# First and last mixer of an eight-stage transformer: blocks of 512 columns, bank pairs in turns, and a one-pass softmax step

## The reference

```
h = x                                        # (256, 1024)
h = h + moba_mixer(rms_norm(h))              # stage A
h = h + conv_ffn(rms_norm(h))                # F0
h = h + mla_mixer(rms_norm(h))               # B
h = h + conv_ffn(rms_norm(h))                # F1
x = x + pool_mixer(rmsnorm(x))               # POOL
x = x + conv_ffn_2(rmsnorm(x))               # F2
x = x + chunk_attention(rmsnorm(x))          # DD
x = x + conv_ffn_2(rmsnorm(x))               # F3
```

## Time and profile before

| what | value |
|---|---|
| median of 3 runs | 1085.82 us (1085.78 to 1086.26) |
| the profiled execution, own time | 1085.73 us |
| its span, first to last instruction | 1083.9 us |
| PE busy with matmuls | 1076.6 us (99%) |
| PE busy with weight loads (overlap) | 973.2 us (90%) |
| DVE / ACT busy | 854.6 us (79%) / 656.8 us (61%) |
| granted TensorE clock | full speed in every slice |
| mean DMA rate | 177 GB/s |
| share of PE in the chain that ended last | 95% |

### The profile page before, as it was taken

One profiled execution on the slowest core, in us unless ns is written; L12 is line 12 of the kernel. 1 busy time (PEld: TensorE's weight loads), 2 busy tenths in 40 slices (PEclk: granted clock), 3 DMA queues, 4 the chain that ended last, 5 costly groups with the idle time before them and its releaser, 6 DMA issues.

```text
span 1083.9 us, 17571 instructions
## 1 busy us (share of the span) xinstructions
PE 1076.6 (99%) x7218; PEld 973.2 (90%) x7218; DVE 854.6 (79%) x1264; ACT 656.8 (61%) x934; POOL 1.3 (0%) x8
## 2 busy tenths in 40 slices
PE   9999999999999999999999999999999999999998
PEld 9998988888898898888889888888999988888888
DVE  7987689877577888988667999776659878998852
ACT  7656557664467775766456577554458765776540
POOL 0000000000000000000000000000000000000000
PEclk9999999999999999999999999999999999999999
DMA  8643256556436045655553366555555443665540
GB/s 310 221 156 118 97 189 229 210 184 215 149 132 224 2 156 223 233 195 184 213 185 117 122 232 229 185 213 186 176 184 180 142 146 126 226 208 193 208 148 30
DMA packets 31951, 191.74 MB, mean 177 GB/s; under 512 B 4480, under 2 KB 5888, under 8 KB 12032
## 3 DMA queue, kind: packets, MB, share of 16 engines
q1 hardware_dynamic: 31872, 190.63, 50.1%
HBM read 189.56 MB, written 1.05 MB: 176 GB/s over the span
## 4 chain that ended last, share of the span: by engine, by line
PE 95%; DVE 2%; ACT 1%; DMA 1%; issue 0%; SPq 0%; DVEq 0%; ACTq 0%
PE banks L414 20%; PE TB L414 12%; PE banks L416 11%; PE SB L414 10%; PE banks L382 8%; PE banks L384 7%; PE banks L383 7%; PE TB L416 6%; PE SB L416 6%; PE banks L581 2%; PE TB L560 1%; PE SB L547 1%; PE SB L937 1%; PE banks L704 1%; DMA raw<-in_a_qkv 1%; PE SB L942 0%
## 5 line engine op out<-in xcount | busy, mean ns | idle before, releaser
L1541 DVE TENSOR_TENSOR wlo<-raw,whi 128x2048 fp32r<-128x2048 f32 (+2 forms) x180 | 395.2, 2200 | 81.1 <-ACT whi L1071 81.0
L1071 ACT ACTIVATE whi<-raw 128x2048 fp32r<-128x2048 f32 (+2 forms) x180 | 330.3, 1839 | 81.9 <-PE banks L416 28.5
L414 PE MATMUL banks<-xx,whi 128*128 128x512 f32 x704 | 247.3, 391 | 0.0
L416 PE MATMUL banks<-xx,wlo 128*128 128x256 f32 x704 | 198.5, 282 | 0.0
L414 PEld LDWEIGHTS banks<-xx,whi 128*128 128x128 f32 x704 | 132.2, 188 | 27.7
L414 PE MATMUL TB<-xx,whi 128*128 128x512 f32 x384 | 135.5, 390 | 0.0
L416 PEld LDWEIGHTS banks<-xx,wlo 128*128 128x128 f32 x704 | 133.1, 189 | 0.1
L382 PE MATMUL banks<-whi,xx 128*128 128x256 f32 (+2 forms) x400 | 116.6, 292 | 1.0 <-DVE wlo L2072 0.8
L384 PE MATMUL banks<-whi,xx 128*128 128x256 f32 (+2 forms) x400 | 113.5, 284 | 0.0
L383 PE MATMUL banks<-wlo,xx 128*128 128x256 f32 (+2 forms) x400 | 113.4, 284 | 0.0
L414 PE MATMUL SB<-xx,whi 128*128 128x512 f32 x320 | 111.8, 390 | 0.0
(11 more groups left out here) (219 smaller groups left out, 2042.2 us busy)
## 6 DMA issues: line engine op xcount, KB each, us to landing
raw<-in_gate SPq DMA_DIRECT2D x44, 1024.0 KB, 4.8
raw<-in_up SPq DMA_DIRECT2D x44, 1024.0 KB, 4.8
raw<-in_down SPq DMA_DIRECT2D x32, 1024.0 KB, 4.8
raw<-in_down SPq DMA_DIRECT2D x16, 768.0 KB, 4.3
raw<-in_d_qkv SPq DMA_DIRECT2D x12, 1024.0 KB, 4.7
raw<-in_a_qkv SPq DMA_DIRECT2D x9, 1024.0 KB, 5.8
raw<-in_a_o SPq DMA_DIRECT2D x4, 1024.0 KB, 4.8
raw<-in_b_o SPq DMA_DIRECT2D x4, 1024.0 KB, 4.7
```

The source lines that it names most:

```text
L414: e.matmul(po[:, 0:512], wh[:, k, sl], a[:, kk, :, :].rearrange("p w s -> p (w s)"), start=start, stop=stop, skip_group_check=True)
L416: return e.matmul(po[:, 0:256], wl[:, k, sl], a[:, kk, 0, :], start=False, stop=stop, skip_group_check=True)
L1071: e.activation(whi[n % RING][:, 0:nk * w], raw[n % RAW][:, 0:nk * w], ACT.Copy).then_inc(s_hi, 1)
L1541: e.tensor_tensor(wlo[n % RING][:, 0:nk * w], raw[n % RAW][:, 0:nk * w], whi[n % RING][:, 0:nk * w].bitcast(F32), ALU.subtract).then_inc(s ...
```

## The change

All of it concerns stages A and DD, but for `shifted` and `exponentials`, which stage B's attention uses as well.

- **Units and slots.** K and Q of four heads are now side by side as 512 columns, V of eight heads likewise. Six slots (K/Q of g=0, V of pairs 0 to 3, K/Q of g=1, 2, 3, V of pairs 4 to 7) take two units each, one for rows 0 to 511 and one for rows 512 to 1023. Slot i fills two banks, one per 128 tokens; the pair of banks is i mod 2. A matmul has 512 moving columns.
- **Order on PE.** Slots 0 and 1 run whole (`both_halves`), with the norm's sums between them; then a slot's quarters (token half x unit) stand between pieces of attention. A turn-over is eight transposes, written into the two banks that the slot itself occupied, and the slot after next waits for ACT's copies out of these banks. `av_bank` and with it the waits of `values` change to suit.
- **Softmax step.** Four `tensor_tensor_reduce` write mask minus scores and its minimum; `exp` takes scale -1 and the minimum as bias. DD's factor 1/8 goes into q's gain.
- **Start.** The order of the quarter loads, splits and squares follows the new units; the constants are loaded after unit 3; `lo(u + 3)` stands behind the norm on DVE.

```diff
+HEAD_SLOTS = (("kq", 0), ("v", 0), ("kq", 1), ("kq", 2), ("kq", 3), ("v", 1))
+KQ_SLOT, V_SLOT = (0, 2, 3, 4), (1, 5)
...
     def qkv(name):
-        for g in range(4):
-            for part in (1, 0, 2):
-                plan.append((name, part * 4 + g, KD, 256))
+        for part, i in HEAD_SLOTS:
+            for half in range(2):
+                plan.append((f"{name}_{part}", 2 * i + half, 4, 512))
...
+                def row_of(i, h, k):
+                    wh, wl = unit(u + 2 * i + k // 4)
+                    sl = slice(h * 128, (h + 1) * 128)
+                    return three(slot_bank(s, i, h)[:, :], xx[:, k, 0, sl], xx[:, k, 1, sl], wh[:, k % 4, :],
+                                 wl[:, k % 4, :], k == 0, k == KD - 1)
+                def quarter(i, h, part):
+                    if h == 0:
+                        weights_here(u + 2 * i + part)
+                    if part == 0:
+                        if i == 3:
+                            e.wait_ge(s_vv, n_vv(s, 0, h))
+                        else:
+                            e.wait_ge(s_te, n_te(s, {2: 0, 4: 1, 5: 2}[i], 1 - h))
+                        if i >= 4 and h == 1:
+                            e.wait_ge(s_ol, n_pair(s, 2 * i - 7 - (s == DD)))
+                    for k in range(4 * part, 4 * part + 4):
+                        last = row_of(i, h, k)
...
+                both_halves(0)
+                norm_sums(s)
+                both_halves(1)
+                turn_over(0)
+                    quarter(2, 0, 0)
+                    quarter(2, 0, 1)
+                    pair_scores(0)
+                    quarter(2, 1, 0)
+                    quarter(2, 1, 1)
...
             def shifted(s, j, scale, mask):
-                e.scalar_tensor_tensor(out=sc[:, :, :], in0=SB[:, :, 0:384], scalar=scale, in1=mask, op0=ALU.mult,
-                                       op1=ALU.add).then_inc(s_msk, 1)
-                e.wait_ge(s_msk, n_pair(s, j))
-                e.tensor_reduce(mxs[:, 0:2], sc[:, :, 0:128], AX_X, ALU.max)
-                kept(e.tensor_reduce(mxs[:, 2:4], sc[:, :, 128:384], AX_X, ALU.max))
-                after_own()
-                e.tensor_scalar(nms, mxs, -1.0, None, ALU.mult).then_inc(s_nmx, 1)
+                for a in range(2):
+                    for h, sl in HALVES:
+                        last = e.tensor_tensor_reduce(sc[:, a, sl], SB[:, a, sl], mask[:, a, sl], -scale, 3e38, ALU.add,
+                                                      ALU.min, low[:, 2 * h + a:2 * h + a + 1])
+                last.then_inc(s_msk, 1)
```

More of the change, by code:

```diff
@@ L444, in last_pair @@
                         last.then_inc(s_half, 1)
[L446 to L454, removed]
             def token_sums(src, dst):
@@ L653, in as_it_comes @@
[L653 to L663, removed]
-                        if (i, k) == (1, 6):
-                            norm_sums(s)
-                    last.then_inc(s_used, 1)
@@ L706, in turn_over @@
-                    last.then_inc(s_turn, 1)
+                    for q in range(2):
+                        b = slot_bank(s, KQ_SLOT[g], q)
+                        if s == DD and q == 1 and g >= 2:
+                            e.wait_ge(s_ol, n_pair(s, 2 * g - 3))
+                        for c in range(2):
+                            at = q * 256 + c * 128
+                            for h in range(2):
+                                last = e.transpose(b[:, c * 256 + h * 128:c * 256 + (h + 1) * 128],
+                                                   nkq[:, h, at:at + 128], ident)
+                        last.then_inc(s_turn, 1)
@@ new lines, in heads_mixer @@
+                    quarter(2, 0, 0)
[3 more added lines that the diff above has]
+                    quarter(2, 1, 1)
+                    pair_scores(1)
+                    quarter(3, 0, 0)
+                    quarter(3, 0, 1)
+                    turn_over(1)
+                    transposes(s, 0)
+                    quarter(3, 1, 0)
+                    quarter(3, 1, 1)
+                    values(s, 0)
+                    transposes(s, 1)
@@ new lines, in heads_mixer @@
+                    pair_scores(2)
+                    quarter(4, 0, 0)
+                    quarter(4, 0, 1)
+                    values(s, 1)
+                    turn_over(2)
+                    transposes(s, 2)
+                    pair_scores(3)
+                    quarter(4, 1, 0)
+                    quarter(4, 1, 1)
+                    values(s, 2)
+                    transposes(s, 3)
+                    pair_scores(4)
+                    quarter(5, 0, 0)
+                    quarter(5, 0, 1)
@@ L751, in heads_mixer @@
+                    values(s, 3)
+                    turn_over(3)
                     transposes(s, 4)
-                    half(3, 2, 1, range(4))
+                    pair_scores(5)
+                    quarter(5, 1, 0)
+                    quarter(5, 1, 1)
+                    transposes(s, 5)
                     pair_scores(6)
-                    half(3, 2, 1, range(4, KD))
+                    rows(0)
+                    values(s, 4)
+                    pair_scores(7)
+                    rows(1, 2)
@@ L804, in heads_mixer @@
-                attention_tail(s, u + 12)
+                    rows(3)
+                    transposes(s, 6)
+                    rows(4)
+                    project(s, u + 12, 2, range(2))
+                    values(s, 6)
+                    transposes(s, 7)
+                    rows(5)
+                    project(s, u + 12, 2, range(2, 4))
+                    values(s, 7)
+                    rows(6)
+                    project(s, u + 12, 2, range(4, 6))
+                    rows(7)
+                    project(s, u + 12, 2, range(6, 8))
@@ L1234, in natural @@
                     e.wait_ge(s_rc, COL[s])
                     if g:
[L1236 to L1241 removed]
+                        e.wait_ge(s_turn, n_turn(s, 2 * g - 1))
```

673 lines of the change are left out of this document (320 added, 353 removed).

## The result

| | before | after |
|---|---|---|
| median, us | 1085.86 (1085.59 to 1086.26, 20 runs) | 1083.63 (1083.15 to 1085.42, 20 runs) |
| profiled execution, own time | 1085.73 | 1083.64 |
| its span | 1083.9 | 1081.8 |
| PE / DVE / ACT busy | 1076.6 / 854.6 / 656.8 | 1074.4 / 833.3 / 654.8 |

The ratio is 0.9981, 95% interval 0.9974 to 0.9988: 2.1 us, and the interval reaches from 1.3 to 2.8 us. The forecast of 1083.6 is met; how it was met is another matter, and most of this part is about that. The medians of the experiments leave out five slow executions, which took 1317 to 5170 us; the intervals are of ratios to the kernel before, run beside each.

The account below looks back on a forecast made before the run. PE, 99% busy, was taken to bound the kernel. Longer matmuls -1.96, gaps -3.5, switches -0.45 and new waits +3.85 summed to -2.1 us, from 1085.73 to 1083.6 us; range 1080.7 to 1087.0.

Parts of the forecast that it names:

- 1. longer matmuls: PE in A and DD: 512-column matmuls replace pairs of 256, winning 3.4 ns per pair, -1.96 us in all.
- 2a. start: Stage A's first 90 matmuls: 1.33 us of PE gaps go, one new wait of 0.5 us comes.
- 2b. wait for Q: Scores of pair 6 in stage A no longer wait for ACT's copy of Q, -0.9 us.
- 2c. rows behind `output_lo(6)`: Projection row after six transposes no longer waits for `output_lo(6)`: 0.45 us in A, 0.80 in DD.
- 3. switches: Fewer PE returns from transposes to projection, 21 to 14 in A, 21 to 16 in DD: -0.45 us.
- 4. norm's sums: Stage A after slot 0: PE newly waits for the last sum of squares, +0.85 us.
- 4. copy of K, A and DD: After `turn_over(0)`, PE waits for ACT to copy V twice, then K: +1.1 us in A, +0.75 in DD.
- 4. DD's chain before transposes 2: After DD's third scores, PE waits for DVE's work through normalization 2, +0.65 us.
- stage A near 117.5 and DD near 116.5 us: Sign expected in the profile after: these lengths for the two rewritten stages, from 119.35 and 117.02 us.
- DVE is not the bound: Softmax step falling from 2.12 to 1.6 us per pair on DVE was worth nothing by itself.
- the slow rival: DVE becomes the bound in A and DD, with a 3.3 us softmax step: +6.9 us, 1090.5 us, chance 0.13.
- the pipeline is later: Margins of 0 to 1 us fail with a 2.4 us softmax step: 1086.0 us, chance 0.17 including no rhythm gain.

Follow-up runs that it names:

- 1.6 us step: Changed kernel with the last of the softmax step's four reductions made twice, a step of 1.58 us: 1086.42 us, ratio 1.0005.
- work behind the step: Changed kernel with an extra DVE addition of 768 columns per pair of heads, placed after the softmax step: 1088.55 us, ratio 1.0022.
- copies first: Changed kernel with ACT copying K and Q ahead of V, in stage A also ahead of unit 6's high part: 1082.83 us, ratio 0.9974.
- turn-over early: Changed kernel with both mixers' first turn-over after seven of slot 1's eight rows, and ACT copying K and Q ahead of V: 1081.79 us, ratio 0.9962.
- two of 256: Changed kernel with every 512-column matmul of K, Q and V made as a pair of 256-column matmuls: 1084.76 us, ratio 0.9990.
- early squares: Changed kernel with stage A's four squares on ACT and their sums on DVE placed between the splits of `x`: 1082.42 us, ratio 0.9970.

## Why the prediction was right, and where it was not

The terms, from the profiled executions (a measured one is the excess of that stretch of PE over its rhythm):

| term | forecast | measured |
|---|---|---|
| 1. longer matmuls | -1.96 | -1.96 |
| 2a. start, against after | -1.33 + 0.5 | +0.08 (1.41 for 1.33) |
| 2b. wait for Q | -0.9 | -0.9 |
| 2c. rows behind `output_lo(6)` | -1.25 | -1.25 |
| small waits of DD, not seen in before | 0 | -0.56 |
| 3. switches, what is left over | -0.45 | -0.17 |
| 4. norm's sums | +0.85 | +0.83 |
| 4. copy of K, A and DD | +1.1, +0.75 | +1.11, +0.74 |
| 4. DD's chain before transposes 2 | +0.65 | 0 |
| sum | -2.1 | -2.1 |

"What is left over" is what closes the sum, not a measurement. By stages the forecast was off both ways: "stage A near 117.5 and DD near 116.5 us" came out at 118.67 and 115.62, 1.2 over and 0.9 under.

**Right by their own steps**: the rhythm, and both waits for K, from the walk of the queues, to 0.01 us. In stage A that closeness holds for this execution: where PE came to the turn-over 1.4 us later, with the old step, it took 1.52 us in place of 1.98.

**The wait for the sums is right by luck.** The prediction has PE done with slot 0 at 17.9 us and the last sum at 18.75. Measured are 18.79 and 19.63: both are 0.9 us late, and only their difference came out. Five more runs share this start and the longer matmuls (old step, 1.6 us step, work behind the step, copies first, turn-over early). In them PE's sums start at 19.21 to 19.83 us, and the waits before them are 0.94 to 1.69 us. The squares were mis-sized as well: the first starts at 14.23 us where 13.7 was forecast, and from there to the end of the last sum it takes 5.25 us (18.79 + 0.69 - 14.23) where 5.0 was. What PE loses in slot 0 it mostly doesn't lose again at the sums, which wait for this chain.

**The start was mis-sized in this execution.** "PE now asks for them at a slower rate; I take one wait a little under the old 0.63" gave 0.5 us; it is 1.41. Of it 0.88 is the wait at 10.32 with its switch, and 0.53 the first two matmuls, which are drawn with 0.77 and 0.57 us and followed by the next after 0.57 and 0.42. Matmuls of 512 start every 0.42 to 0.43 us where a window reads 0.50 (22 to 24 us with ACT's copies first), so a lowered clock is a guess; here the windows read 1.00 from 6 to 8 us. In the same five runs the excess of slot 0 is 0.46 to 0.97 us. Start and sums together were forecast at 1.35 us; they are 2.24 here and 1.6 to 2.6 in the five.

**The step that failed** is "DVE is not the bound, so the 0.5 us saved a pair is worth nothing by itself", and with it the threshold of the slow rival, "it decides from 2.5 us a step". The matrix:

| | old step, 2.12 us | 1.58 us | new step, 1.12 us |
|---|---|---|---|
| old order | 1085.9 | | 1084.0 |
| new order | 1092.5 | 1086.4 | 1083.6 |

The threshold came from a balance of totals: 17.4 us of PE against 12.4 of DVE and two steps. DVE's list runs in order and waits inside it (with the old step, 2.0 us for ACT's squares in the third group and 5.1 for the first scores), so it cannot use the whole 17.4; with the old step its group is 16.6 us of work, 0.8 under PE's, and the kernel loses 8.9 us. A busy share or a sum per group is a bound from below and no threshold. The walk, which looked at each deadline, did see one wait of 0.65 us in DD at 1.6 us a step; the run at 1.58 us shows 0.66 at the same third turn-over, one place earlier than named, and another 2.2 us elsewhere: 0.5 in the rest of DD, 0.86 in stage A's tail, both passed as "in time", and 0.85 in the latent mixer, which was costed at nothing.

So two errors cancelled. Had the step cost the 1.6 us that the prediction took, the change would have given 1086.4 us, no gain, the rival called "the pipeline is later". It came out at 1083.6 because the step was cheaper than the price taken. Of the prices in hand (1.5, 1.6, 2.4 and 3.3) none was low enough, the lowest because the instructions that write the minimum were charged 0.1 to 0.2 us each; they are drawn with 0.08 and cost nothing beside their neighbours. The step of 2.4 us that the prediction supposes for that rival is shown by no run: the changed kernel's takes 1.12, and its fused pass of 256 columns is drawn with 0.42 us, as is a plain subtraction of that size.

**What the gain is made of**, then, depends on the order of counting. The step alone gives -2.0 us in the old order. Blocks, slots and pipeline add -0.4 to that, which can't be told from nothing: the intervals of the two ratios (0.9973 to 0.9991 and 0.9974 to 0.9988) lie on one another. Counted the other way, the new order alone costs 6.5 us and the step wins 8.9. In the changed kernel the longer matmuls win 1.96 us and three new waits (2.7 us) take it back; the place of four squares, an order on ACT and an earlier turn-over on PE remove them. The forecast credited the new order alone with the 0.9 us of the wait for Q, which each edit removes by itself, and with 0.36 of the 0.80 before the last transposes, which the step removes by itself.

## What to carry to other kernels

When a change shortens an engine that isn't the bound, don't price it by its slack in total: go through its list and count the places where the bound engine waits for it, and try the short step in the old order first. When an instruction is merged away and a wait for a result in the same bank takes its place, look at what stands ahead of that copy on the copying engine. And when one trace agrees with a walk to 0.02 us, compare the two ends of the wait as well, in more than one execution: here both ends were 0.9 us late.

## What the runs showed of the hardware

The granted clock fell to 0.50 in runs of the new order; the profile of before has a mean of 1.000. In four profiled executions PE waited 1.1 to 1.5 us for the norm's sums, behind the waits of the start (old step 1.12, copies first 1.52, 1.6 us step 1.49, work behind the step 1.48), and slot 1 of stage A then ran for some 3 us at half rate; in those with waits of 0.67 to 0.9 us (the changed kernel 0.67, turn-over early 0.78, two of 256 0.86), or with none, it did not. From the run with ACT's copies first:

```profile
19.45 0.80 PE L456 MATMUL SB<-ones,ssum 128*128 128x1 f32 x6 [1.52 <-DVE ssum L1566]
```

```profile
20.00:22.00 2.00, 2.00 (x10) 1.67 (x10) 1.25 (x8) 0.90 (x1) 0.00 (x0) 0.75 1.02 368
22.00:24.00 2.00, 2.00 (x6) 1.56 (x5) 1.86 (x6) 1.89 (x1) 0.00 (x0) 0.50 0.98 396
24.00:26.00 2.00, 2.00 (x9) 1.60 (x9) 1.97 (x6) 0.02 (x1) 0.00 (x0) 0.90 0.17 70
```

Slot 1 takes 12.82 us in place of 11.27, 1.55 more, so the wait of 1.52 costs twice its length. In the changed kernel this happens in some executions: its 20 runs spread over 2.3 us where before has 0.7, and the three slowest (1085.42, 1084.29 and 1084.27 us) have a mean granted clock of 0.998, the others 0.999 to 1.00. Only one of the 20 was traced in full, so that it is the same place in the three is inferred. With the squares early and the turn-over moved up, five runs lie within 0.3 us.

The length of a wait doesn't decide it alone. With the old step the clock fell behind the 1.91 us before 105.92; behind 1.65 us at the same place, with the work behind the step, it did not (windows again):

```profile
105.65 0.88 PE L583 MATMUL banks<-pt,vv 128*64 128x128 f32 x12 [1.65 <-DVE ox L1790]
```

```profile
106.00:108.00 2.00, 2.00 (x24) 1.83 (x21) 1.06 (x4) 1.01 (x2) 0.00 (x0) 1.00 0.03 12
```

Nor did it fall behind the 1.94 us for K in the kernel with early squares:

```profile
34.00:36.00 2.00, 2.00 (x11) 1.60 (x10) 1.61 (x1) 0.00 (x0) 0.00 (x0) 1.00 1.07 438
```

What else decides isn't shown. A wait thus cost more than its length in these runs (1.52 + 1.55 us with the copies first, 1.12 + 1.57 with the old step), and removing it can be worth as much.
